# Moving the feature scales of a norm into the next projection's weights, and its per-token factor from VectorE to ScalarE

## The reference, cut to what matters

```python
    # end of the first block
    h = h + hier_moe(...)
    x = rmsnorm(h, final_norm_g)
    # start of the second block
    h = rms_norm(x, mix_norm[i])              # x / sqrt(mean(x^2) + eps) * g
    y = conformer_conv(h, a_w_in[j], a_b_in[j], ...)

def conformer_conv(x, w_in, b_in, conv_w, conv_b, ln_g, ln_b, w_out, b_out):
    a, g = jnp.split(x @ w_in + b_in, 2, axis=-1)
    h = a * jax.nn.sigmoid(g)
    h = lax.conv_general_dilated(h, conv_w, ...) + conv_b     # 31 taps, per channel
    h = jax.nn.silu(layer_norm(h, ln_g, ln_b))
    return h @ w_out + b_out
```

## Time and profile before

| | |
|---|---|
| Time, median of 3 runs | 2143.92 us (2139.66 to 2144.05) |
| Profiled execution: its own time | 2141.92 us |
| Its span, first to last instruction | 2140.1 us |
| Mean granted TensorE clock | 0.967 of full speed |
| PE busy | 1966.5 us (92%), 11159 matmuls |
| DVE busy | 1605.0 us (75%), 1700 instructions |
| ACT busy | 1054.4 us (49%), 1395 instructions |
| POOL busy | 555.1 us (26%) |
| JOIN stage | about 1148 to 1224 us of the span |
| Conv stage | about 1246 to 1416 us |

### The profile page before, as it was taken

One profiled execution on the slowest core, in us unless ns is written; L12 is line 12 of the kernel. 1 busy time (PEld: TensorE's weight loads), 2 busy tenths in 40 slices (PEclk: granted clock), 3 DMA queues, 4 the chain that ended last, 5 costly groups with the idle time before them and its releaser, 6 DMA issues. The chain is left out here.

```text
span 2140.1 us, 30097 instructions
## 1 busy us (share of the span) xinstructions
PE 1966.5 (92%) x11159; PEld 1061.1 (50%) x11159; DVE 1605.0 (75%) x1700; ACT 1054.4 (49%) x1395; POOL 555.1 (26%) x348
## 2 busy tenths in 40 slices
PE   6988989889499999999994899949899999999999
PEld 5775436645245544445543555534444444444444
DVE  6865637753789999999987746474696898889876
ACT  5332326732368888888875545474322323322320
POOL 2221130000023333333320001012022565556430
PEclk9999999999699999999997999979999999999999
DMA  6111320042289999999997446437101212121111
GB/s 241 40 40 40 112 56 1 1 168 92 77 321 417 402 422 406 402 400 396 403 364 303 158 149 240 144 100 271 40 1 40 79 40 77 41 78 39 59 59 79
DMA packets 80979, 363.69 MB, mean 170 GB/s; under 512 B 13992, under 2 KB 27944, under 8 KB 48312
## 3 DMA queue, kind: packets, MB, share of 16 engines
q1 hardware_dynamic: 61704, 309.64, 36.9%
q0 software_dynamic: 18640, 52.53, 7.1%
q10 hardware_dynamic: 544, 0.26, 0.0%
HBM read 337.21 MB, written 37.75 MB: 175 GB/s over the span
## 5 line engine op out<-in xcount | busy, mean ns | idle before, releaser
L432 PE MATMUL ps<-split,xt 128*128 128x512 f16 (+1 forms) x776 | 291.0, 375 | 5.2 <-issue 4.6
L649 DVE SCALAR_TENSOR_TENSOR split<-stage,split 128x2048 f16<-128x2048 f32 x128 | 289.5, 2283 | 7.1 <-ACT split L645 5.4
L433 PE MATMUL ps<-split,xt 128*128 128x512 f16 (+1 forms) x776 | 290.8, 375 | 0.0
L434 PE MATMUL ps<-split,xt 128*128 128x512 f16 (+1 forms) x776 | 290.5, 374 | 0.0
L645 ACT ACTIVATE split<-stage 128x2048 f16<-128x2048 f32 x128 | 240.5, 1904 | 95.4 <-PE ps L434 95.4
L1395 POOL TENSOR_TENSOR stage<-stage 128x1024 f32<-128x1024 f32 x52 | 145.2, 2793 | 264.8 <-DVE split L858 261.8
L432 PE MATMUL ps<-xt,split 128*128 128x512 f16 (+1 forms) x528 | 189.6, 359 | 9.8 <-issue 8.2
L433 PE MATMUL ps<-xt,split 128*128 128x512 f16 (+1 forms) x528 | 189.2, 358 | 0.0
L434 PE MATMUL ps<-xt,split 128*128 128x512 f16 (+1 forms) x528 | 189.0, 358 | 0.0
L649 DVE SCALAR_TENSOR_TENSOR arena<-arena 128x2048 f16<-128x2048 f32 x64 | 146.3, 2287 | 3.1 <-ACT arena L645 3.1
L853 ACT ACTIVATE split<-stage 128x1024 f16<-128x1024 f32 x56 | 57.3, 1048 | 136.0 <-PE pt L434 72.9
(11 more groups left out here) (540 smaller groups left out, 4813.1 us busy)
## 6 DMA issues: line engine op xcount, KB each, us to landing
stage<-in_w_gate SPq DMA_DIRECT2D x64, 1024.0 KB, 7.3
stage<-in_w_up SPq DMA_DIRECT2D x64, 1024.0 KB, 7.6
arena<-in_w_down SPq DMA_DIRECT2D x64, 1024.0 KB, 8.2
stage<-in_w_mlp SPq DMA_DIRECT2D x32, 1024.0 KB, 4.9
stage<-in_w_dense_a SPq DMA_DIRECT2D x16, 1024.0 KB, 8.4
arena<-in_conv_taps POOLq DMA_DIRECT2D x22, 640.0 KB, 5.3
stage<-in_w_dense_b SPq DMA_DIRECT2D x12, 1024.0 KB, 12.1
resid<-in_x SPq DMA_DIRECT2D x16, 512.0 KB, 4.8
```

The source lines that it names most:

```text
L432: nc.tensor.matmul(out_ap, lh, rh, start=start, stop=False)
L433: nc.tensor.matmul(out_ap, lh, rl, start=False, stop=False)
L434: return nc.tensor.matmul(out_ap, ll, rh, start=False, stop=stop)
L649: nc.vector.scalar_tensor_tensor(out=wlo(s), in0=wstage(s), scalar=WS, in1=whi(s), op0=ALU.mult, op1=ALU.subtract).then_inc(s_wo[s], 1)
```

## The change

The norm's feature scale `g` multiplies feature by feature what then is multiplied with the rows of `w_in`, so it can be applied to the rows of `w_in` instead. In the transposed layout a row of a weight unit is a partition, so the scale is one number per partition and block: the split of units 0 to 7 becomes four instructions of 512 columns on each engine, each with its own column of `g2w = 64 * g`. The column table `g2` (8 columns) is appended to the conv tables, which are loaded in the place of the 512 KB broadcast, and DVE multiplies it by 64 once, before `lo_b(2)`.

What is left of the second norm, the factor of each token, is applied by ACT in a new step `scale:t`. DVE keeps the reciprocal. In ACT's list `scale:t` follows `two:t`, directly from tile 2 on.

```diff
+        g2 = tables[:, 16 + 3 * NCG:24 + 3 * NCG]
+        b64, g2w = Z[:, 1176:1184], Z[:, 1184:1192]
...
+            if m < 8:
+                act.wait_ge(s_g2, 2)
+                for kk in range(UK):
+                    c, k = slice(kk * UC, kk * UC + UC), m % 2 * UK + kk
+                    i = nc.scalar.activation(b_hi(m)[:, c], wstage(s)[:, c], ACT.Copy, scale=g2w[:, k:k + 1])
+                i.then_inc(s_wh[s], 1)
+            else:
+                nc.scalar.activation(b_hi(m), wstage(s), ACT.Copy, scale=WS).then_inc(s_wh[s], 1)
...
+            if m < 8:
+                for kk in range(UK):
+                    c, k = slice(kk * UC, kk * UC + UC), m % 2 * UK + kk
+                    i = nc.vector.scalar_tensor_tensor(out=b_lo(m)[:, c], in0=wstage(s)[:, c], scalar=g2w[:, k:k + 1],
+                                                       in1=b_hi(m)[:, c], op0=ALU.mult, op1=ALU.subtract)
+                i.then_inc(s_wo[s], 1)
...
-        JOIN_ACT = seq("one:0 one:1 two:0 two:1 hi:0 hi:1 one:2 two:2 one:3 hi:2 two:3 hi:3 one:4 two:4 one:5 hi:4 "
-                       "two:5 gate:0 one:6 hi:5 two:6 gate:1 one:7 hi:6 two:7 hi:7 gate:2 taps:0 taps:1 gate:3 taps:2")
+        JOIN_ACT = seq("one:0 one:1 two:0 two:1 scale:0 scale:1 hi:0 hi:1 one:2 two:2 scale:2 one:3 hi:2 two:3 scale:3 "
+                       "hi:3 one:4 two:4 scale:4 one:5 hi:4 two:5 scale:5 gate:0 one:6 hi:5 two:6 scale:6 gate:1 one:7 "
+                       "hi:6 two:7 scale:7 hi:7 gate:2 taps:0 taps:1 gate:3 taps:2")
...
-            sp.dma_start(gm, a["gains"][3:4, :].to_broadcast([P, D])).then_inc(s_gain, 16)
+            sp.dma_start(tables, a["conv_tables"]).then_inc(s_gain, 16)
             for m in (2, 3, 0, 1):
                 load_b(sp, m)
             overflow(sp, over)
-            sp.dma_start(tables, a["conv_tables"]).then_inc(s_tab, 16)
...
+                elif what == "scale":
+                    act.wait_ge(s_g2, t + 3)
+                    xn_wait(act, 3, t)
+                    nc.scalar.activation(xn[:, t % 2, :], H[:, t, :], ACT.Copy, scale=rstd[:, t:t + 1]).then_inc(s_xn, 1)
...
+                    dve.wait_ge(s_gain, 64)
+                    nc.vector.tensor_scalar(g2w, g2, WS, None, ALU.mult).then_inc(s_g2, 1)
+                    dve.wait_ge(s_g2, 2)
                     for m in (2, 3, 0, 1):
                         lo_b(dve, m)
...
             def second_norm(u):
                 dve.wait_ge(s_std, stats_count("two", u))
-                ch.done(nc.vector.reciprocal(rstd[:, u:u + 1], std[:, u:u + 1]))
-                xn_wait(dve, 3, u)
-                nc.vector.scalar_tensor_tensor(out=xn[:, u % 2, :], in0=H[:, u, :], scalar=rstd[:, u:u + 1],
-                                               in1=gm, op0=ALU.mult, op1=ALU.mult).then_inc(s_xn, 1)
+                nc.vector.reciprocal(rstd[:, u:u + 1], std[:, u:u + 1]).then_inc(s_g2, 1)
```

More of the change, by code:

```diff
@@ L172, in build @@
         rb = Z[:, 576:612]
-        gm = Z[:, 1280:2304]
         WORK = AR[:, 8192:12288]
@@ L190, in build @@
         wO = AR[:, 0:2048]
-        tables = Z[:, 0:16 + 3 * NCG]
+        tables = Z[:, 0:24 + 3 * NCG]
         b_in = tables[:, 0:16]
         cb, lng, lnb = [tables[:, 16 + NCG * i:16 + NCG * i + NCG] for i in range(3)]
-        b64 = Z[:, 208:216]
+        g2 = tables[:, 16 + 3 * NCG:24 + 3 * NCG]
+        b64, g2w = Z[:, 1176:1184], Z[:, 1184:1192]
         blk = cols[:, 320:448]
@@ L213, in build @@
         mean, msq, var, rdev = [WORK[:, 2304 + MC * i:2304 + MC * i + MC] for i in range(4)]
-        bo = gm
+        bo = Z[:, 1280:2304]
         HTh = AR[:, 0:2048].bitcast(F16).rearrange("p (k t) -> p k t", k=4)
@@ L299, in build @@
         s_rmix = sem("ret_mix")
-        s_lam = sem("lambda")
+        s_lam = s_g2 = sem("lambda_or_second_norm_factors")
         s_lx = sem("lambda_exp")
@@ L705, in hi_b @@
                 act.wait_ge(s_full[g % 4], g // 4 + 1)
-            nc.scalar.activation(b_hi(m), wstage(s), ACT.Copy, scale=WS).then_inc(s_wh[s], 1)
+            if m < 8:
[6 more added lines that the diff above has]
+                nc.scalar.activation(b_hi(m), wstage(s), ACT.Copy, scale=WS).then_inc(s_wh[s], 1)
         def lo_b(dve, m):
@@ L710, in lo_b @@
             dve.wait_ge(s_wh[s], r + 1)
-            nc.vector.scalar_tensor_tensor(out=b_lo(m), in0=wstage(s), scalar=WS, in1=b_hi(m),
-                                           op0=ALU.mult, op1=ALU.subtract).then_inc(s_wo[s], 1)
+            if m < 8:
[4 more added lines that the diff above has]
+                i.then_inc(s_wo[s], 1)
+            else:
+                nc.vector.scalar_tensor_tensor(out=b_lo(m), in0=wstage(s), scalar=WS, in1=b_hi(m),
+                                               op0=ALU.mult, op1=ALU.subtract).then_inc(s_wo[s], 1)
         def group_b(pe, g, units, feature_major, ft, tk):
@@ L1694, in gate @@
                 if p == 0:
-                    act.wait_ge(s_tab, 32)
+                    act.wait_ge(s_tab, 16)
                 nc.scalar.activation(ub[p % 2], tokens_by_phase(g), ACT.Sigmoid, bias=b_in[:, 8 + k:9 + k],
@@ L2173, in gated @@
                 if p == 0:
-                    dve.wait_ge(s_tab, 32)
+                    dve.wait_ge(s_tab, 16)
                     ch.done(nc.vector.tensor_scalar(b64, b_in[:, 0:8], WS, None, ALU.mult))
@@ L2233, in out_tile @@
                     dve.wait_ge(s_x[t], 80)
-                    dve.wait_ge(s_tab, 48)
+                    dve.wait_ge(s_tab, 32)
                     ch.done(nc.vector.tensor_tensor(H[:, t, :], H[:, t, :], bo, ALU.add))
@@ L3005 @@
         "conv_tables": np.concatenate([by_channel(f["a_b_in_2"]), by_phase(f["a_conv_b_2"]),
-                                       by_phase(f["a_ln_g_2"]), by_phase(f["a_ln_b_2"])], axis=1),
+                                       by_phase(f["a_ln_g_2"]), by_phase(f["a_ln_b_2"]),
+                                       by_channel(f["mix_norm_2"])], axis=1),
         "conv_taps": taps_layout(f["a_conv_w_2"][0]),
```

## The result

The changed kernel is slower. Its median is 2149.64 us (2142.95 to 2152.07, 20 runs) against 2141.72 us for the kernel before (2136.66 to 2144.48, 20 runs, on the same chip): ratio 1.0038, 95% interval 1.0032 to 1.0045, or 8.1 us more (6.9 to 9.6). The forecast was 9.0 more, which lies in that interval. In absolute terms it was 2152.9, 3.3 above the measured median: 2.2 of these come from its starting point, a median of 3 runs of the kernel before (2143.92), the rest from the sum. One run of experiment 1 took 2694.21 us at a mean granted clock of 0.741 and is not in its ratio. The profiled execution has a span of 2148.3 us against 2140.1, so 8.2 more, at a mean granted clock of 0.965.

What follows compares the result with a forecast made beforehand. TensorE, busy 92% of the span, was taken as the bound, losing time only where it waits. Join 3.8, unit 5 1.8 and clock 1.7 twice sum to 9.0 us, onto median 2143.92 giving 2152.9; range 2146.5 to 2156.

Steps and rivals of the forecast that it cites:

- gate 0's product on DVE: Join: table load and sigmoid follow scale:5 on ACT, so DVE's product starts at 1199.62 against 1195.66, +3.96 us.
- the join term: Join, tile 6: its transposes start 3.8 us later, bounds 3.3 and 4.3, and the conv part inherits this.
- tile 7's xn: Join: xn 7 ready near 1220.7, PE there at 1221.6, so covered; without the cover a further 2 us.
- four pieces, ACT and DVE: Weight splits: four pieces take 2.56 us against 1.90 on ACT and 2.76 against 2.29 on DVE.
- conv wait: Second conv block: PE's idle for the taps split on DVE grows from 2.15 to 3.95 us.
- last expert's second output copy: Last expert: the copy queued behind the splits of units 2 and 3 moves from 1137.58 to at most 1137.8.
- later waits swallow the delay: Rival, conv stage: with transfers standing still in time PE only idles less there, 2143 to 2147 us; chance 0.12.
- low end: Likeliest case (both clock losses) with its low terms 3.3, 0.7 and 1.7: 2149.6 us.
- unit 5 term: Conv stage: unit 5's pieces, queued behind the gate, delay the sums and taps split by 1.8 us, low bound 0.7.
- The clock term: Behind PE's idle before tile 6 and in the conv block: 1.7 us lost at each place, bounds 0 and 2.4.
- The clock fell at both places: Against the rival that the clock holds at one or both: 5.6 to 7.3 us, 2149.5 to 2151.2; chance 0.27.
- DVE was not the bound: Against the rival that DVE bounds the join: PE's waits before tiles 4 and 6 vanish, 2139.9 us; chance 0.06.

Runs made afterwards that it cites:

- experiment 1: Changed kernel with the per-token factor back on VectorE as a column multiplication and ACT's order of before, pieces kept: ratio 1.0007 against the kernel before.
- 4: Changed kernel with ACT's sigmoids of gates 0 and 1 ahead of scale:5 and scale:6: ratio 1.0019 against the kernel before.
- 2: Changed kernel with units 0 to 7 split by one instruction each at a constant scale, feature scale left out: ratio 1.0017 against the kernel before.
- experiment 3: Changed kernel with ACT's copy of unit 5 moved ahead of its part of the gate of pair 7: ratio 1.0017 against the kernel before.
- 7: Changed kernel with 56 overwritten matmuls ahead of tile 6's transposes and of the awaited conv group: ratio 1.0022 against the kernel before.
- experiment 8: Changed kernel with the per-token factor on VectorE and units 0 to 7 split plainly, feature scale left out: ratio 0.9993 against the kernel before.
- 9: Kernel before with unit 5's copy early and overwritten matmuls ahead of tiles 0, 4 and 6 in the join: ratio 0.9986 against the kernel before.
- 10: Changed kernel with the factor on VectorE, unit 5 early, and filler matmuls ahead of tiles 0, 4, 6 and the conv group: ratio 0.998 against the kernel before.
- experiment 6: Kernel before with ACT's copy of unit 5 directly behind that of unit 4: ratio 0.9993 against the kernel before.
- experiment 5: Changed kernel with the factor on VectorE and unit 5's copy early, pieces kept: ratio 0.9996 against the kernel before.
- 12: 10 plus filler matmuls in the u_rows and z_rows waits and ahead of the last norm's tile 7: 2134.04 us, ratio 0.997 against the kernel before.
- 11: 9 plus filler matmuls in the u_rows and z_rows waits and ahead of the last norm's tile 0: ratio 1.0001 against the kernel before.

## Why the prediction was right, by its own steps

| Step of the prediction | predicted | measured |
|---|---|---|
| scale copy on ACT | 1.12 us | 1.15 |
| tile 4's transposes | +0.8 | +1.21, 0.32 of it from ahead of the stage |
| tile 5's | +1.2 | +1.64, likewise |
| gate 0's product on DVE | +3.96 | +4.43, likewise |
| tile 6's (the join term) | +3.8 | +4.28, so 3.96 of its own |
| tile 7's xn | covered, 0.9 to spare | covered, 2.3 to spare (ready 1221.2, PE there 1223.5), 1.44 of it from the clock |
| four pieces, ACT and DVE | 2.56, 2.76 | 2.54, 2.74 |
| conv wait | 2.15 to 3.95 | 2.15 to 3.81, +1.66 |
| clock, each place | +1.7 | +1.44 and +1.66 |
| later waits | swallow 0 | swallow 0.9 |
| last expert's second output copy | at most 1137.8 | 1138.94 |

The 0.32 come from DVE's adds of tile 1, at 1152.63 against 1152.32, which wait for y_rows. That this is so little is luck: the expert rows were stored 1.36 us later (1140.48 against 1139.12), and landed faster by 1.05. The prediction had bounded the second output copy at 1137.8 because it looked only at ScalarE's splits; they ended at 1137.07, as forecast, but the copy then waited 1.39 us for PE, whose clock had fallen (see the last section). The clock loss behind tile 6 is 12.73 - 11.29 us between the transposes of tiles 6 and 7. In the conv block PE is 7.55 late at the wait and 9.21 late when it comes to its wait for u_rows (1415.38 - 7.71 is 1407.67, before 1398.46).

**The one term that was off** is the last: "later waits swallow the delay" was a rival with 0.12 and a term of nothing in the sum. The u_rows wait shrank from 8.44 to 7.71, and the shift fell from 9.21 to 8.48 and then to 8.2 at the end. The rest comes with PE, as the prediction held against that rival. This is read from one pair of profiles, and 0.9 us is less than the interval of the measured difference. The forecast's low end also counts the clock once where both losses are assumed (3.3, 0.7, 1.7); with both it is 2151.3, not 2149.6. Nothing in the range hangs on it.

**The join term** is shown by experiments 1 and 4: taking `scale` off ACT gives back 6.6 us, and putting the two sigmoids ahead of it 4.0, with 0.82 instead of 3.79 us of idle before tile 6. **The unit 5 term** is shown by 2 and 3, which agree at 4.5 us against the changed kernel. I had put 3.5 on wait and clock together; the difference from 4.5 is within the intervals. **The clock term** is shown by 7: 3.4 us for both places, by prediction 3.4, and 3.1 by the distances in the profiles.

**On the table load** the Trainium skill and the trace differ once more. The load starts at 1198.02, as the scale copy ends at 1198.00, and the sigmoid 1.29 later. The Trainium skill ("ScalarE: Activation LUTs", What ACT_TABLE_LOAD costs) adds 1.38 us for a drain. By an estimate from that figure the join term would have been 5.2; it was 3.96, and no row here shows the drain.

**The rivals.** The clock fell at both places. DVE was not the bound: its eight instructions went and tile 4 came later; even in experiment 8, where the shorter instruction stays on DVE and ACT has no copies, the 4.2 us saved there did not all come back. Where VectorE keeps the factor, its instruction is 0.53 us shorter. The Trainium skill ("VectorE: DVE Perf Modes", Mode 2×_2P) says that `tensor_scalar`, with one tensor source in SBUF, gets twice the rate even in fp32; the 0.75 against 1.28 us of experiment 1 are a factor of 1.7 for the whole instruction, so they agree in the main. This shorter instruction, on VectorE, is the part of the change that could have paid. What it is worth, about 1 us by the profiles of experiments 9 and 10, is not clear of noise in any measured time.

## What to carry to other kernels

When two engines hand a tile back and forth, price a move between them by its place in the receiving engine's order, not by its busy time: ACT was half idle and the copies no dearer than what they replaced, yet 8 us were lost, 4 of which came back with two sigmoids moved ahead. Splitting an instruction into pieces costs only where somebody waits for the last piece, so look for that one unit and move it, rather than cheapen all. And look at the granted clock behind each idle stretch of PE: cheap matmuls that end just before the awaited data arrive gave 3.4 us in the changed kernel, and 1.5, 3.4 and 2.1 in the other three comparisons (experiments 9 against 6, 10 against 5, 12 against 10; in the first and the last the intervals overlap, and 12 took 6.4 off the kernel before in all), but they must stand exactly where PE idles.

## What the runs showed of the hardware that was not expected

**An idle stretch of about 2 us sometimes costs the clock and sometimes not.** The conv wait of all fourteen profiles, with the distance from the awaited group to PE's wait for u_rows, in which PE does the same work in all of them:

| idle before the conv group | kernels | clock just behind it | group to u_rows wait |
|---|---|---|---|
| 3.81 | changed, 4 | 0.50 | 119.46, 119.43 |
| 3.81 | 1 | 0.50 | 120.26 |
| 2.15 | before, 2 | 1.00 | 117.80, 117.81 |
| 2.15 | 8 | 0.50 | 119.44 |
| 1.96 | 3 | 1.00 | 117.80 |
| 1.96 | 5 | 0.50 | 119.45 |
| 0.95 or 0.96 | 6, 9, 11 | 1.00 | 117.82, 117.81 (6, 9) |
| 0.68, filled | 7 | 1.00 | 117.81 |
| 0.17, filled | 10, 12 | 1.00 | 117.81 (10) |

Experiment 8's wait, then the clock behind it and behind the 1.96 us of experiment 3 (from 1284.59), columns as in the earlier trace rows:

```profile
1277.13 0.23 PE L2811 MATMUL pt<-arena 128*128 128x128 f16 x1 [2.15 <-DVE gb L2185]
```

```profile
1278.00:1279.00 1.00, 1.00 (x12) 1.00 (x11) 1.00 (x1) 1.00 (x3) 0.54 (x1) 0.50 0.40 118
```

```profile
1285.00:1286.00 1.00, 1.00 (x22) 1.00 (x20) 1.00 (x3) 1.00 (x3) 0.44 (x1) 1.00 0.34 101
```

So the prediction's sentence that the present 2.15 costs no clock was true of two of the three executions with that length; in the third it cost 1.6 us. That can explain why experiment 5 fell short of its forecast, and part of why executions of one kernel lie 9 us apart (2142.95 to 2152.07), but which share of its executions lose the clock no profile tells. Experiment 6, which kept its clock in the conv block, lost it before tile 6, where it idled 1.97 us: tile 7's transposes follow 12.97 us behind, against 11.29 in the kernel before.

```profile
1203.16 1.09 PE L487 MATMUL pt<-misc,xn 128*128 128x128 f32 x8 [1.97 <-DVE xn L2156]
```

```profile
1205.00:1206.00 1.00, 1.00 (x4) 0.30 (x2) 0.15 (x1) 0.98 (x3) 0.00 (x0) 0.50 0.00 0
```

**The same happened ahead of the join.** In the last expert PE waits 2.15 us for DVE in both profiles. In the kernel before it resumed at full clock, in the changed kernel at half, and the store of the expert rows left 10.63 us behind ScalarE's copy ahead of the weight splits instead of 9.04. First the kernel before, then the changed one:

```profile
1132.18 0.39 PE L432 MATMUL pt<-arena 128*128 128x512 f16 x1 [2.15 <-DVE arena L2114]
```

```profile
1131.95 0.61 PE L432 MATMUL pt<-arena 128*128 128x512 f16 x1 [2.15 <-DVE arena L2132]
```

It does not come from the change: of the fourteen profiles eleven have the longer distance (10.6 to 10.7 us), among them those of experiments 9 and 11, which are the kernel before in this part, and three the shorter (9.0 to 9.1), among them that of experiment 1 with its splits in pieces.

**The way back varies too.** In the kernel before and in experiment 6 PE resumes after 22.18 and 21.11 us of idle and then does the same work. Windows of the kernel before, then of experiment 6, columns as in the earlier trace rows:

```profile
1170.00:1171.00 1.00, 1.00 (x6) 0.72 (x5) 0.96 (x2) 1.00 (x2) 0.00 (x0) 0.50 1.07 430
1171.00:1172.00 1.00, 1.00 (x10) 0.83 (x8) 0.94 (x3) 0.29 (x1) 0.00 (x0) 0.90 0.98 389
```

```profile
1165.00:1166.00 1.00, 1.00 (x7) 0.67 (x6) 1.00 (x2) 0.78 (x1) 0.00 (x0) 0.50 1.02 415
1166.00:1167.00 1.00, 1.00 (x8) 0.77 (x7) 0.96 (x2) 0.66 (x3) 0.00 (x0) 0.67 1.03 422
```

In the first the clock rises some 11.4 us after the transposes of tile 0, in the second 9.0, and tile 4's transposes come 29.2 and 28.0 us behind tile 0's. The 2.76 us of idle before tile 4, on which the prediction leaned, is 1.09 in experiment 6. The Trainium skill ("TensorE: Matmul & The Clock Gate", Part 1: The HAM clock gate) says that the same kernel shows different numbers of slow matmuls from run to run; these two executions, of kernels that do the same up to here, agree. For a reader of profiles it means that a difference of 1 to 2 us between two single executions, before tile 4 or behind a wait of 2 us, is not yet one between two kernels.
